# Weight halves split one tile sooner, a normalisation's turn in three steps, a router on the eight-largest instructions, and expert weights in eight buffers

## The reference

```
for layer in range(2):
    h = h + 0.5 * rmsnorm(swiglu(rmsnorm(h, g[0]), w_ffn_in[layer, 0], w_ffn_out[layer, 0]), g[1])
    mix = gla_mixer(...) if layer < 1 else swa_mixer(...)      # gated linear attention / sliding window
    h = h + rmsnorm(mix, g[3])
    h = h + 0.5 * rmsnorm(swiglu(rmsnorm(h, g[4]), w_ffn_in[layer, 1], w_ffn_out[layer, 1]), g[5])
```

```
x   = layer_norm(ALPHA * h + mixed, ln1_g, ln1_b)
ffn = hier_moe(x, ...)                                         # 32 experts, 4 groups of 8
x   = layer_norm(ALPHA * x + ffn, ln2_g, ln2_b)
# hier_moe: grp = argmax(g_logits); top 2 of the 8 experts of that group;
# weight = softmax(top 2) * softmax(g_logits)[grp]; expert = (silu(x@gate) * (x@up)) @ w_down
```

## Time and profile before

| | us |
|---|---|
| median of 3 runs | 1790.23 (1789.76 to 1792.95) |
| the profiled execution | 1788.14 |
| its span, first to last instruction | 1786.2 |
| PE busy in it | 1735.2 (97%) |
| DVE busy | 1059.4 (59%) |
| ACT busy | 723.9 (41%) |
| mean granted clock of PE | 0.993 of 2.4 GHz |

### The profile page before, as it was taken

One profiled execution on the slowest core, in us unless ns is written; L12 is line 12 of the kernel. 1 busy time (PEld: TensorE's weight loads), 2 busy tenths in 40 slices (PEclk: granted clock), 3 DMA queues, 4 the chain that ended last, 5 costly groups with the idle time before them and its releaser, 6 DMA issues.

```text
span 1786.2 us, 31558 instructions
## 1 busy us (share of the span) xinstructions
PE 1735.2 (97%) x12364; PEld 1402.7 (79%) x12364; DVE 1059.4 (59%) x1910; ACT 723.9 (41%) x1171; POOL 21.2 (1%) x26
## 2 busy tenths in 40 slices
PE   8999999999999999999999999999999999999996
PEld 8999989899999999997799999998953333333332
DVE  6775475687755877659787657867672222222223
ACT  5444463464444544456654446857331101110110
POOL 0000000100000000000000001000020000000000
PEclk9999999999999999999999999999999999999998
DMA  6545334435453355542245545442879999999996
GB/s 237 188 167 192 136 122 162 60 142 188 177 205 137 133 182 183 192 142 89 95 166 194 216 175 191 142 157 104 335 289 397 427 427 428 427 428 427 427 428 260
DMA packets 42337, 409.67 MB, mean 229 GB/s; under 512 B 5304, under 2 KB 5304, under 8 KB 7056
## 3 DMA queue, kind: packets, MB, share of 16 engines
q1 hardware_dynamic: 40032, 402.21, 58.0%
q0 software_dynamic: 1936, 5.79, 1.6%
q10 hardware_dynamic: 288, 0.52, 0.1%
HBM read 405.87 MB, written 2.63 MB: 229 GB/s over the span
## 4 chain that ended last, share of the span: by engine, by line
PE 83%; DVE 7%; DMA 6%; ACT 2%; issue 1%; DVEq 0%; SPq 0%; ACTq 0%
PE ps L592 81%; DMA soon<-w_gate_up 4%; DMA raw<-w_units 2%; PE ps L596 2%; DVE w_lo L1746 2%; ACT w_hi L1286 1%; DVE rs L1788 1%; DVE h L1855 0%; DVE x_lo L1806 0%; DVE x_lo L1808 0%; DVE m_low L2460 0%; ACT arena L1541 0%; DVE h L1859 0%; DVE arena L2043 0%; DVE std L1793 0%
## 5 line engine op out<-in xcount | busy, mean ns | idle before, releaser
L592 PE MATMUL ps<-x_hi,w_hi 128*128 128x256 f32 (+1 forms) x2144 | 614.7, 287 | 16.2 <-DVE w_lo L1746 5.4
L592 PE MATMUL ps<-x_lo,w_hi 128*128 128x256 f32 (+1 forms) x2144 | 610.2, 285 | 0.0
L592 PE MATMUL ps<-x_hi,w_lo 128*128 128x256 f32 (+1 forms) x2144 | 608.9, 284 | 0.0
L1746 DVE TENSOR_TENSOR w_lo<-raw,w_hi 128x1024 fp32r<-128x1024 f32 (+1 forms) x352 | 447.0, 1293 | 145.5 <-ACT w_hi L1286 145.0
L1286 ACT ACTIVATE w_hi<-raw 128x1024 fp32r<-128x1024 f32 (+1 forms) x352 | 384.4, 1113 | 203.3 <-PE ps L592 137.5
L592 PEld LDWEIGHTS ps<-x_hi,w_hi 128*128 128x128 f32 x2144 | 403.8, 188 | 24.3 <-issue 11.6
L592 PEld LDWEIGHTS ps<-x_hi,w_lo 128*128 128x128 f32 x2144 | 405.4, 189 | 0.0
L592 PEld LDWEIGHTS ps<-x_lo,w_hi 128*128 128x128 f32 x2144 | 404.6, 189 | 0.2
L592 PE MATMUL ps<-hid_hi,w_hi 128*128 128x272 f32 (+1 forms) x720 | 206.0, 286 | 0.8 <-DVE hid_lo L1808 0.4
L592 PE MATMUL ps<-hid_hi,w_lo 128*128 128x272 f32 (+1 forms) x720 | 204.6, 284 | 0.0
L592 PE MATMUL ps<-hid_lo,w_hi 128*128 128x272 f32 (+1 forms) x720 | 204.0, 283 | 0.0
(11 more groups left out here) (339 smaller groups left out, 1945.8 us busy)
## 6 DMA issues: line engine op xcount, KB each, us to landing
raw<-w_units SPq DMA_DIRECT2D x144, 1024.0 KB, 4.8
soon<-w_gate_up SPq DMA_DIRECT2D x34, 2048.0 KB, 18.1
late<-w_gate_up SPq DMA_DIRECT2D x30, 2048.0 KB, 17.9
raw<-w_out_units SPq DMA_DIRECT2D x32, 1408.0 KB, 6.3
soon<-w_down SPq DMA_DIRECT2D x16, 2048.0 KB, 18.2
late<-w_down SPq DMA_DIRECT2D x16, 2048.0 KB, 18.1
bias_rows<-kT POOLq DMA_DIRECT2D x1, 1536.0 KB, 33.4
cst<-table SPq DMA_DIRECT2D x1, 1448.0 KB, 11.8
```

Of the source, the lines that this page charges most:

```text
L592: return nc.tensor.matmul(out_ap, lhsT, rhs, start=start, stop=stop, skip_group_check=True)
L1746: v.tensor_tensor(part(w_lo, c, 0, n), raw_slot(u, j * n, n), part(w_hi, c, 0, n).bitcast(F32), ALU.subtract).then_inc(lo_made, 1)
```

## The change

1. **Weight halves.** At the boundaries of `gout` and `sout` (two tiles to a unit) ACT and DVE split one half more behind each odd tile, so that every half of the following units is split one tile sooner. In `in0` DVE splits unit 2 before it waits for the first root. In `in2` the hidden tile 0 is made ahead of the first half of unit 3. The first half of `v` is split before the exponentials of the gate.
2. **The turn** is three instructions: the reciprocal after tile 2, the product of four tiles after tile 3, and that of the other four after tile 4.
3. **`r`**: ACT copies raw tile 0 to `acc`, a buffer of its own, before it takes the root; DVE scales it from there.
4. **`pb` and `wo`**: DVE splits the halves of `pb` and `wo` in smaller steps between its tiles; ACT copies `pb` tiles 4 to 7 out of their banks, and DVE multiplies them with the gates from memory.
5. **Router**: `max` and `max_index` (the eight largest of a row with their places) replace `first_max`. One pair of each finds the group, one more pair both experts. The blocks' table loses two instructions, the slots come from four product-and-sum instructions; `m_P` is written row block by row block, with a signal after the first (`p_begun`); PE gathers the first row block of groups 0 and 1 on that signal. All of `rows_low` stands in front of the count of the quads. The products with zeros are 1 and 2 in place of 4 and 3.
6. **Experts**: eight buffers. The new one lies over `zg` and its neighbours, and piece 7 is issued as soon as the last `wo` operand is made. All pieces up to 83 go round eight buffers, in loops whose body is two quads (eight experts, 24 pieces) on PE and on SP; only the last quad or later ones read their expert numbers. ALPHA * x is added after quad 6 in place of quad 3. The rows of ln1 go to `cst`, and those of ln2, which take the same place, are loaded when POOL has used the former.

```
-    for _ in range(4):
-        mm(ps[0][:, :], m_zero, cst[:, 0:512], False, False)
+    mm(ps[0][:, :], m_zero, cst[:, 0:512], False, False)
...
     sp.wait_ge(lo_made, 2 * N_UNITS)
     load_ahead(4)
+    sp.wait_ge(x_ready, 12 * KT)
+    load_ahead(7)
     t = plan["wo"][1].at(7)
     sp.wait_ge(full[t[0]], t[1] + 1)
     load_ahead(5)
     load_ahead(6)
-    for piece in range(7, 6 * EXP_UNITS):
...
+    for piece in range(N_ROOMS, QUAD_PIECES):
+        load_piece(piece // EXP_UNITS, piece % EXP_UNITS, piece % N_ROOMS, piece - N_ROOMS + 2)
+    with sp.Fori(0, FIXED // 2) as lap:
+        for piece in range(QUAD_PIECES, QUAD_PIECES + TURN):
+            load_piece(8 * lap + piece // EXP_UNITS, piece % EXP_UNITS, piece % N_ROOMS,
+                       TURN * lap + piece - N_ROOMS + 2)
...
     pool.wait_ge(x_ready, 12 * KT)
-    pool.dma_start(zg[:, 0:2 * D], ln1_rows.to_broadcast([P, 2 * D])).then_inc(ln1_in, 16)
-    t = plan["wo"][1].at(7)
-    pool.wait_ge(full[t[0]], t[1] + 1)
-    pool.dma_start(m_g, rows[:, 1024:2048]).then_inc(ln2_in, 16)
-    pool.dma_start(m_b, rows[:, 2048:3072]).then_inc(ln2_in, 16)
+    pool.dma_start(cst[:, at:at + 2 * D], ln1_rows.to_broadcast([P, 2 * D])).then_inc(ln1_in, 16)
...                                             (the four products with m_lg and m_lb of both halves)
+    pool.wait_ge(x2_ready, 2)
+    pool.dma_start(m_g, rows[:, 1024:2048]).then_inc(ln2_in, 16)
+    pool.dma_start(m_b, rows[:, 2048:3072]).then_inc(ln2_in, 16)
...
+    with pe.Fori(0, FIXED // 2) as lap:
+        next_quad(1, lap)
+        next_quad(2, lap)
     for p in range(2):
         pe.wait_ge(x2_ready, p + 1)
         for n in range(2):
             mm(ps[2 * p + n][:, :], m_alpha, m_o[:, p * D + n * 512:p * D + (n + 1) * 512], False, False)
...
-    split_to(u0 + m // per + 1)                               # branch_out (ACT), residual (DVE)
+    split_to(u0 + m // per + 1, 2 if per == 1 else 2 + m % 2)
...
     if m == 2 and n > 1:
-        turn_back(w)
+        turn_inverse(w)
+    if m in (3, 4) and n > 1:
+        turn_back(4 * (m - 3), w)
...
     sum_squares(TA)
+    split_to(plan["in0"][0] + 2)
     inverse_rms(0, TA)
...
-    def first_max(x, n, top, tmp, one):
-        then(v.tensor_reduce(top, x, AX, ALU.max))
...
+    def largest(x, top, at):
+        for p in range(2):
+            did(v.max(two(r_[top])[:, p], x[:, p]))
+        for p in range(2):
+            own(chain[0] - 1 if p == 0 else None)
+            last = did(v.max_index(two(r_[at])[:, p].bitcast(U32), two(r_[top])[:, p], x[:, p]))
+        own(last)
```

More of the change, by code:

```diff
@@ L54 @@
 PIECE = 2 * UNIT
-PIECE_PARTS = 1
+QUAD_PIECES = 4 * EXP_UNITS
 C_COLS = {}
@@ L498, in load_piece @@
                 src = src.rearrange("a (p k) n -> p a k n", k=4)
[L499 to L504, removed]
+                if begun is not None:
+                    sp.wait_ge(exp_begun, begun)
+                sp.dma_start(piece_rooms[room].rearrange("p (a k n) -> p a k n", a=1, k=4), src).then_inc(e_landed[room], 16)
             def load_ahead(piece):
@@ L520, in _ @@
             load_ahead(6)
-            for piece in range(7, 6 * EXP_UNITS):
[L523 to L528, removed]
-            sp.wait_ge(table_ready, 1)
[L530 to L536, removed]
+            for piece in range(N_ROOMS, QUAD_PIECES):
[4 more added lines that the diff above has]
+                               TURN * lap + piece - N_ROOMS + 2)
+            sp.wait_ge(table_ready, 1)
+            n_quads = sp.value_load(meta_i[0:1, MAXB:MAXB + 1], min_val=NE // 4, max_val=MAXB // 4)
+            with sp.Fori(FIXED, n_quads) as quad:
+                for n in range(QUAD_PIECES):
+                    if n % EXP_UNITS == 0:
+                        e = sp.value_load(meta_i[0:1, bass.ds(4 * quad + n // EXP_UNITS, 1)], min_val=0, max_val=NE - 1)
+                    room, use, _ = more_rooms(n)
+                    held = n - 5 if use == 2 else (n + 5 if n < 4 else 8 if n == 4 else n) - QUAD_PIECES
+                    load_piece(e, n % EXP_UNITS, room, QUAD_PIECES * quad + held + 2)
             for p in range(2):
@@ L1162, in combine, with expert, arrived @@
                 return m
-            def expert(quad, s, gathers=True):
+            def expert(quad, s, lap=0, gathers=True, more=False):
+                n = EXP_UNITS * s if more else QUAD_PIECES * quad + EXP_UNITS * s
+                quad = quad if more else quad + 2 * lap
                 b = 4 * quad + s
-                def arrived(i, g):
-                    piece = EXP_UNITS * s + i
-                    if isinstance(quad, int):
-                        room, use = piece % N_ROOMS, 16 * (piece // N_ROOMS + 1)
-                    else:
-                        room = loop_rooms[piece % (2 * EXP_UNITS)]
-                        use = 32 * quad + 16 * (piece // (2 * EXP_UNITS)) + (16 if 4 * EXP_UNITS - N_ROOMS > room else 0)
-                    pe.wait_ge(e_landed[room][g], use)
+                def arrived(i):
+                    if more:
+                        room, use, each = more_rooms(n + i)
+                        first = FIXED * QUAD_PIECES
+                        use = 16 * (first // N_ROOMS + (room < first % N_ROOMS) + use - each * FIXED) + 16 * each * quad
+                    else:
+                        room, use = (n + i) % N_ROOMS, 16 * ((n + i) // N_ROOMS + 1) + 16 * (TURN // N_ROOMS) * lap
+                    pe.wait_ge(e_landed[room], use)
                     return piece_rooms[room]
@@ L1252, in _ @@
                     mm(ps[2 * p + n][:, :], m_alpha, m_o[:, p * D + n * 512:p * D + (n + 1) * 512], False, False)
-            quads(NE // 8, n_quads)
-            expert(n_quads - 1, 3, False)
+            pe.wait_ge(count_ready, 1)
+            n_quads = pe.value_load(meta_i[0:1, MAXB:MAXB + 1], min_val=NE // 4, max_val=MAXB // 4)
+            with pe.Fori(FIXED, n_quads) as quad:
+                expert(quad - 1, 3, more=True)
+                for s in range(3):
+                    expert(quad, s, more=True)
+            expert(n_quads - 1, 3, gathers=False, more=True)
             pe.wait_ge(yhi_made, 4 * n_quads)
@@ new lines, in _ @@
+            then(v.scalar_tensor_tensor(e4, r_["g1"].rearrange("p (a g n) -> p a g n", a=2, n=1).to_broadcast([P, 2, 4, 8]), NEG, e4,
+                                        ALU.mult, ALU.add))
+            largest(em, "top", "at")
+            for k in range(2):
+                did(v.tensor_tensor(two(r_[("o1", "o2")[k]]), C("iota", 0, 32).rearrange("p (a n) -> p a n", a=1).to_broadcast([P, 2, 32]),
+                                    two(r_["at"])[:, :, k:k + 1].bitcast(U32).to_broadcast([P, 2, 32]), ALU.is_equal))
```

250 lines of the change are left out of this document (139 added, 111 removed).

## The result

The changed kernel takes 1772.8 us (median of 6 runs, 1771.16 to 1776.41) against 1790.56 before (6 runs): a ratio of 0.9902 (95% interval 0.989 to 0.9914), 17.8 us less. The forecast was 1776, in a range of 1771 to 1784. The profiled execution takes 1771.16, its span is 1769.2: 17.0 less than before, where 14.0 were forecast. All executions here were in the chip's faster state but one of 5479.78 us in the first experiment, which ratios leave out.

What follows compares the result with a forecast made beforehand. The DMA stream of expert pieces was taken to set the end, with PE the bound ahead of the experts. The terms summed to -14.0, from 1790.2 to 1776 us, range 1771 to 1784.

Steps and rivals of the forecast that it cites:

- Rival A: Experts: if PE ends last or the DMA engines idle at the restart, piece 7's 4.9 goes; 1781 us, chance 0.12.
- `in0`: In `in0`: PE's 3.03 us wait for a low half of unit 2 goes; -3.0, bounds 0 and -3.0.
- `in2`: In `in2`: PE's 1.02 us wait for a bank freed behind a split goes; -1.0, bounds 0 and -1.0.
- `gout` and `sout`: At both: the split freeing the raw slot comes sooner, shortening the wait for the last square; -1.0 each, bounds 0 and -2.4.
- `r` and `v`: Waits of 0.95 and 0.97 go, a stall of 1.3 comes in `v`; -0.6, bounds +0.5 and -1.9.
- `pb` and `wo`: Bank wait and low clock go (3.8), partly becoming two waits of 0.9 in `wo`; -1.6, bounds +1.7 and -3.8.
- Router: Router: `m_ready` 2.1 sooner, gathers 2.9 sooner, expert 0 3.4 sooner; -3.4, bounds -0.8 and -4.5.
- Rival C: Router: `max` and `max_index` take 0.5 each, nothing won up to `m_ready`; 1779 us, chance 0.09.
- The stream: Experts: piece 7 loaded ahead -4.9, rows of ln2 in the full stream +2.45, loops and eight buffers 0.
- some 5 us: Sign in the experts: the DMA engines' idle stretch before the restart would be some 5 us, with share 1.0 after it.
- Rival B: Ahead of the experts other waits take over: only `in0` of the 8.2 holds, one more lost before `wo`; 1784, chance 0.10.
- Rival D: Experts: the doubled loop bodies load code in each lap, so the kernel is slower; over 1795 us, chance 0.05.

Runs made afterwards that it cites:

- the first experiment: The kernel before with two edits only, the earlier split of unit 2 in `in0` and the earlier hidden tile 0 in `in2`: 1785.12 us, ratio 0.9968.

## Why the prediction was right, and where it was not

**What sets the end.** Right: three runs changed the stream (one piece, the rooms, the rows), and first to last silu followed each, while PE kept something to spare. Rival A is out. It would come next: with the ln2 rows gone PE has 3.9 - 2.5 = 1.4 left.

**`in0`, `in2`, `gout`, `sout`.** The mechanisms were right, confirmed alone (`in0`, `in2`) or by undoing the turn. The size was off: -7.1 for the four where -6.0 was forecast, and -3.3 and -1.3 lie beyond the bounds set for `in0` and `in2`. One cause is that I took a wait at the length that the trace prints. Removing it returns 0.26 more. The products behind the wait at 26.98 of the kernel before show why:

```profile
27.21 0.29 PE L592 MATMUL ps<-x_lo,w_hi 128*128 128x272 f32 x1
27.34 0.29 PE L592 MATMUL ps<-x_hi,w_lo 128*128 128x272 f32 x1
```

In a full row products are 0.13 apart and each prints as 0.29, so the last one before a wait sticks out by 0.16; the first behind it needs 0.23 to its successor, 0.10 more than in a row. For `in0` and `in2` that is the whole miss, 0.5 of the 1.1 by which the four terms were short. At `gout` and `sout` the waits that went whole are others than the one that the forecast names:

```profile
363.44 0.39 PE L592 MATMUL ps<-x_hi,w_hi 128*128 128x272 f32 x1 [0.91 <-DVE w_lo L1746]
...
878.06 0.39 PE L592 MATMUL ps<-x_hi,w_hi 128*128 128x256 f32 x1 [0.97 <-DVE w_lo L1746]
```

The wait for the last square is nearly all still there (0.34 and 0.82 for 1.34). What was won is the shift of the whole chain, as forecast, but 1.4 and 1.1 of it and not 1.0 each; why it is more was not taken apart.

**`r` and `v`.** Forecast -0.6, measured -0.7; the stall foreseen in `v` is 0.48 and not 1.3, and one of 0.73 for the gate's product, which I did not foresee, stands beside it at 237.11.

**`pb` and `wo`.** This term failed: -1.6, measured -0.1. The landing was right (1290.02 to 1279.16 is 10.9 sooner, of which 9.2 were brought along: 1.7), and so was what the new waits cost, 2.2. But they came as one wait of 2.00 and not as two of 0.9, and what I had set aside as the upper bound came true: behind it the clock was 0.50 from 1283 to 1286, and that ate the 1.6 that was left. With the queue ahead of the unit shortened both vanish and the 3.8 that I had counted as gross gain is there (3.7).

**Router.** `m_ready` comes 2.1 sooner counted from the start of the statistics, as forecast, and the instructions are cheap: 0.12 to 0.15 for a maximum (half of a pair), 0.25 and 0.27 for a search with its load of values; the eight take 1.6, where 1.4 was assumed. Rival C is out. The signal `p_begun` is 2.9 sooner, as forecast. PE was not there: its last zeros ran at 0.50 until 1302.78. The step that failed is "three fewer make room for that": they did, but waits of 0.68 and 0.43 took their place, and the low clock behind them held up the last zeros; filling the waits returned 1.1 us.

**The stream.** Forecast -2.45, measured -5.5. The price of a piece and of the rows was right. "With the same pattern of issues" was wrong twice: the six rooms left a hole of 3.3 at 1368 that I had not looked for, since I read the rate from 1400 on ("SP has three pieces outstanding"), and the eight buffers have none there (share 1.00 from 1368 to 1376). Taken in the order of the runs: rows of ln2 in the old rooms (with ALPHA * x moved) +0.1, rooms -1.6, piece 7 -4.0. The sign of "some 5 us" of idle DMA engines was off as well: from the last landing in the trace to the issue of the restart it was 1323.67 - 1314.12 = 9.55 before and is 1312.11 - 1304.97 = 7.14. That is piece 7's 4.9 less and 2.45 more, since the rows of ln2 have left this stretch; the sign had forgotten them.

**Rival B.** Ahead of the router 7.9 of its 8.2 us came, so it is out. Its time was not derived: with `in0` kept the sum is -8.9, and no row supports the 3.0 that its -5.9 then takes for "one more" wait.

**Rival D.** The loops of two quads load no code to speak of. The queues from 1400 to 1500, for the earlier trace rows:

```profile
q1 hardware_dynamic: 2939, 42.71, 100.5%
q8 instruction: 2, 0.03, 0.1%
```

From 1320 to 1750 it is 8 packets with 0.13 MB against 6 with 0.10 before. By the rule of the Trainium skill (Runtime: NRT & Kernel Launch, "Instruction fetch mechanics") PE's body of some 1,100 instructions stays loaded, and the trace agrees.

**Luck.** Ahead of the experts -11.6 was forecast and -11.6 measured, with 1.5 missing at `wo` and 1.1 in the router, and 1.2 more in the waits and 1.3 in the sliding window. The 1.3 in the sliding window is the clock's: it was 0.50 there for 6.8 us in the profile before and for 3.4 in the one after. Nine profiles here share the changed kernel's instructions up to that point, and seven of them have 3.4, two 6.8; both profiles with the old instructions have 6.8, so that the change has no part in it is not shown. The -11.6 itself is that of one pair of executions: in the repeat of the changed kernel the same part is 4.05 longer, which leaves -7.5, and the medians (17.8 less, 5.5 of it in the stream) put it at -12.3.

## What to carry to other kernels

Look for holes over the whole stream, not at its steady part: a queue that is full in the mean can run dry once, and bytes that come into such a hole cost little (0.1 here, 2.5 in the full stream). When an early wait goes, ask which landing is late next, and what stands in its queue: moving two transfers behind the last weight gave 3.7, as much as part 4 was to give before its new waits. A short wait of PE is worth its length, a quarter of a us, and what a lower clock, if one follows, takes from the products behind it; fill it or remove it. And compare parts, not totals, where two executions of one kernel differ by 4 us.

## What the runs showed of the hardware

In the router of the changed kernel two waits of 0.68 and 0.43 us within 2 us, between products of 32 columns, came ahead of a granted clock of 0.50 (1.2 GHz) that held for 3.4 us in one execution and 6.8 in another. All eight profiles with these waits have it; in the two with the waits filled by products with zeros the clock stayed at 1.00. PE was busy throughout the low stretch itself.

That the waits alone bring it is not shown. In the kernel before with the edits of `in0` and `in2` the clock fell in the router too, behind the same thin products and a wait of only 0.17, where the profile of the kernel before has 1.00:

```profile
1308.00:1311.00 3.00, 3.00 (x6) 1.21 (x4) 2.79 (x13) 0.00 (x0) 0.00 (x0) 0.50 0.62 255
```

There it cost expert 0 some 0.1: the zeros that it slowed ran where PE otherwise waits 0.81. It costs 1.1 where the gathers are ready early.

A wait of 1.8 to 2.1 in `pb` or `wo` was followed by 0.50 in all ten profiles that have one, and the two without one have none there. But length does not decide it: behind the wait of 3.03 in `in0` the clock of the kernel before stayed at 1.00.

```profile
24.00:36.00 12.00, 9.02 (x72) 9.02 (x73) 11.32 (x21) 5.38 (x7) 0.00 (x0) 1.00 0.42 145
```

Stretches of low clock ahead of the experts come and go between executions of the same kernel: those of the changed kernel's two profiles differ by 4.1 us in time (1771.16 and 1775.26) with the same instructions, while first to last silu repeats to 0.01 us.

Two `max` in a row take 0.24 on 128 x 8 and 0.29 on 128 x 32; `max_index` is two instructions, 0.09 and 0.16 (0.18 on 32 columns).
